# Eight sample states of a decoder layer: outer products on TensorE, or scaled copies on ScalarE and one addition on VectorE

## The chip, the cores and the metric

The kernel runs on one core of one Trainium2 chip. The metric is the device time of one execution in microseconds (us); smaller is better. A core has TensorE (PE in the profile, its weight loads PEld), VectorE (DVE), ScalarE (ACT), GpSimd (POOL) and SyncE (SP), each with its own queue of instructions that run in order. They meet at semaphores only. Data lie in SBUF (128 partitions) and in PSUM, where TensorE writes; DMA queues move data between memory and SBUF.

## The reference, cut to what matters

One layer of a hybrid decoder runs on a prompt of 256 tokens and on 8 samples of one new token each. For the samples the recurrence is a single step per head (8 heads, state 128x128, `f`, `k`, `q` and `v` of 128 numbers per head and sample):

```python
q = silu(q_raw) * 128 ** -0.5
fg = lb + (1 - lb) * sigmoid(f_raw)
k = 1 - fg
S_new = fg[:, None] * S + k[:, None] * v[None, :]     # one state per head and sample
o = q @ S_new
```

`S_new` for all 8 samples and 8 heads is an output (4 MB), and `o` goes on into the head's norm, the gate, the output projection and the rest of the layer.

## The kernel before, in words

All products are made from float32 split into two float16 halves: ScalarE makes the high half of a weight block (L610), VectorE the low half (L977), and TensorE adds three products per pair of tiles. The weights stream through in blocks of 512 KB: SyncE loads a block into one of 4 raw slots, ScalarE and VectorE split it into one of 8 slots, TensorE uses it. ScalarE and VectorE split block `b + 4` in their turn for block `b` (`AHEAD = 4`). Blocks 0 to 79 are the input projection (`S_IN`): ten groups of 8 blocks, each group four tiles of 128 columns for all 264 tokens, 24 products of 0.11 us per block. Group 0 and 3 give q, 1 and 4 f (and k), 2 and 5 v, 6 and 7 the gate g, 8 and 9 u. In a group's last block (7, 15, 23, 31, 39, ...) `evict_in` takes the four tiles out of PSUM: for f, q and g ScalarE makes the sigmoid (`gates`, L621 to L625) and VectorE the product (L1139, L1140, L1145, L1148); the first product of the next group needs the tile of that number free (or, after f, its sigmoid made).

Beside this stream the mixer is woven in, by block numbers. `QUAD_AT = (17, 41)` starts the prompt recurrence of heads 0 to 3 and 4 to 7: every second block TensorE makes the scores of one level (L2081), for which VectorE multiplies q and k (`level`, L1168) and ScalarE packs the keys (`pack_keys`, L717); at +9 and +11 v is turned (L2041), at +16 to +22 follow cross scores, keys, outputs o (L2120, taken by L749 and L751) and final states (L2133, L756, stored by L759). `SAMPLE_AT = (26, 38, 50, 58)` starts the sample states of a pair of heads. With `r` the blocks since then:

- `sample_halves` (VectorE, blocks 24 and 48) splits k and v of the samples into halves in `kv_wide`, four float16 columns of each, and q into `q16`.
- r = 0: TensorE turns them (`sample_kv`, 8 turns of L2030, one between two stream products), ScalarE copies the result to `kv_smp` (L768).
- r = 2 and 4: TensorE makes 8 outer products of four rows each (`outer`, L2055) in two PSUM banks; VectorE makes `state * f + product` (`pair_states`, L1187), 8 instructions of 128x128.
- r = 5 and 6: ScalarE makes the high half of the new state (L776), r = 6 and 7: VectorE the low half (L1280); r = 10: TensorE the 32 small products with q (`os`, L2169 and L2170).
- GpSimd stores the new state and loads that of the next pair into the same two buffers.

Jobs beside the stream share four PSUM banks in turn; the table `JOBS` says who empties each. In_jobs of a block stand behind its sixth stream product. After o of the last pair: mean (L1410), root on ScalarE (`ROOT_AT = 65`, with a table load, L825), Newton step, `o_normalised` (L1320) and the turn of o at blocks 68, 70, 72 and 74 (L2210).

## Time and profile before

| | |
|---|---|
| median of 3 runs | 1169.81 us (1169.33 to 1170.16) |
| the profiled execution | 1170.06 us, of which span 1168.2 us, granted clock 0.998 |
| busy: PE, PEld | 1156.9, 1037.3 us |
| busy: DVE, ACT, POOL | 1006.4, 565.1, 55.5 us |
| L977, low half of a block, on DVE | 414 times, 1.22 us; two in a row start 1.14 us apart |
| L610, high half, on ACT | 414 times, 1.05 us |
| L1187, state times f plus product, on DVE | 64 times, 17.2 us in all |
| L759, issue of a store on ACT's queue; L825, table load | 0.43 us; 1.28 us |
| mean DMA rate | 201 GB/s |

How to read it: PE is an engine that is busy nearly all the time, so what matters of the others is when each delivers. An instruction's duration reaches from its start to its end, but two in a row overlap by some 0.1 us: what a string of them costs is the distance between starts. The span begins with the first instruction of the program; the profiled execution's own time holds 1.9 us around it.

### The profile page before, as it was taken

The numbers are of one execution on the slowest core, as the hardware profiler recorded it, in microseconds if no ns is written. First come the engines' busy times: TensorE is split into PE (matmuls) and PEld (weight loads), VectorE is DVE, ScalarE is ACT, GpSimd is POOL, SyncE is SP. The second block draws the span as 40 slices with busy tenths as digits, with TensorE's granted clock in tenths as the row PEclk, the third lists the DMA queues.
The fourth block names the chain that finished last, engine by engine and source line by source line (L and its number), as shares of the span: only waits on it lengthen the run. The fifth ranks groups of instructions, "written<-read, shape, count | busy, mean of one in ns | idle before, by whom it ended". The sixth has DMA issues, their size and how long they took to land.

```text
span 1168.2 us, 31003 instructions
## 1 busy us (share of the span) xinstructions
PE 1156.9 (99%) x12469; PEld 1037.3 (89%) x12469; DVE 1006.4 (86%) x1575; ACT 565.1 (48%) x810; POOL 55.5 (5%) x80
## 2 busy tenths in 40 slices
PE   8999999999999999999999999999999999999997
PEld 7888888888888899899998999989989999999886
DVE  6778799778867898998989989888899999998687
ACT  6545645654546644444444444444444444444443
POOL 2122310100000200000000000000000000000000
PEclk9999999999999999999999999999999999999999
DMA  8767876766566566666666666666666666667561
GB/s 253 238 200 207 237 217 192 232 190 190 181 211 199 180 216 199 195 194 204 215 200 195 194 202 215 203 193 194 201 199 215 202 199 207 206 199 242 163 190 75
DMA packets 193385, 234.92 MB, mean 201 GB/s; under 512 B 8010, under 2 KB 153777, under 8 KB 193040
## 3 DMA queue, kind: packets, MB, share of 16 engines
q1 hardware_dynamic: 187984, 221.08, 60.4%
q0 software_dynamic: 3968, 11.89, 3.6%
q8 instruction: 53, 0.87, 0.3%
q10 hardware_dynamic: 1360, 0.92, 0.3%
q14 instruction: 20, 0.16, 0.0%
HBM read 226.89 MB, written 7.43 MB: 201 GB/s over the span
## 4 chain that ended last, share of the span: by engine, by line
PE 93%; DVE 4%; ACT 1%; issue 1%; DMA 0%; DVEq 0%; ACTq 0%
PE acc L2322 13%; PE acc L1924 10%; PE acc L1926 10%; PE acc L1928 10%; PE acc L2363 7%; PE acc L2325 6%; PE acc L2324 6%; PE acc L2303 6%; PE acc L2305 6%; PE wrk L2303 4%; PE wrk L2305 4%; PE acc L2365 2%; PE acc L2366 2%; DVE hl L977 2%; PE wrk L2081 1%
## 5 line engine op out<-in xcount | busy, mean ns | idle before, releaser
L977 DVE SCALAR_TENSOR_TENSOR hl<-raw,hl 128x1024 f16<-128x1024 f32 x414 | 493.7, 1220 | 51.7 <-ACT hl L610 49.0
L610 ACT ACTIVATE hl<-raw 128x1024 f16<-128x1024 f32 x414 | 420.3, 1051 | 168.8 <-DMA raw<-in_w_down_dram 88.0
L2322 PE MATMUL acc<-nrm,hl 128*128 128x264 f16 x1344 | 274.8, 276 | 0.3 <-DVE tg L1481 0.3
L1926 PE MATMUL acc<-nrm,hl 128*128 128x264 f16 x920 | 253.9, 276 | 0.0
L1928 PE MATMUL acc<-nrm,hl 128*128 128x264 f16 x920 | 253.9, 276 | 0.0
L1924 PE MATMUL acc<-nrm,hl 128*128 128x264 f16 x920 | 253.9, 276 | 0.0
L2324 PE MATMUL acc<-nrm,hl 128*128 128x264 f16 x672 | 185.5, 276 | 0.0
L2325 PE MATMUL acc<-nrm,hl 128*128 128x264 f16 x672 | 185.5, 276 | 0.0
L2322 PEld LDWEIGHTS acc<-nrm,hl 128*128 128x128 f16 x1344 | 129.0, 98 | 18.1 <-DVE tg L1481 0.6
L2363 PE MATMUL acc<-big,hl 128*128 128x264 f16 x704 | 130.2, 276 | 0.0
L1924 PEld LDWEIGHTS acc<-nrm,hl 128*128 128x128 f16 x920 | 90.2, 98 | 13.2 <-issue 0.3
L1928 PEld LDWEIGHTS acc<-nrm,hl 128*128 128x128 f16 x920 | 90.3, 98 | 12.8
L1926 PEld LDWEIGHTS acc<-nrm,hl 128*128 128x128 f16 x920 | 90.3, 98 | 12.4
L2363 PEld LDWEIGHTS acc<-big,hl 128*128 128x128 f16 x704 | 66.9, 98 | 8.8
L2325 PEld LDWEIGHTS acc<-nrm,hl 128*128 128x128 f16 x672 | 65.8, 98 | 9.8
L2324 PEld LDWEIGHTS acc<-nrm,hl 128*128 128x128 f16 x672 | 65.8, 98 | 9.5
L1924 PE MATMUL acc<-mix,hl 128*128 128x264 f16 x256 | 70.7, 276 | 0.7 <-DVE hid L1357 0.7
L2365 PE MATMUL acc<-big,hl 128*128 128x264 f16 x256 | 70.7, 276 | 0.0
L2366 PE MATMUL acc<-big,hl 128*128 128x264 f16 x256 | 70.7, 276 | 0.0
L1928 PE MATMUL acc<-mix,hl 128*128 128x264 f16 x256 | 70.7, 276 | 0.0
L1926 PE MATMUL acc<-mix,hl 128*128 128x264 f16 x256 | 70.7, 276 | 0.0
L876 ACT ACTIVATE xe<-wrk 128x132 f32<-128x132 f32 x21 | 5.9, 282 | 109.5 <-PE acc L2305 109.5
(492 smaller groups left out, 2241.9 us busy)
## 6 DMA issues: line engine op xcount, KB each, us to landing
raw<-in_w_gate_up_dram SPq DMA_DIRECT2D x168, 512.0 KB, 4.6
raw<-in_w_down_dram SPq DMA_DIRECT2D x88, 512.0 KB, 4.0
raw<-in_w_in_dram SPq DMA_DIRECT2D x80, 512.0 KB, 4.7
raw<-in_w_out_dram SPq DMA_DIRECT2D x32, 512.0 KB, 5.0
raw<-in_w_ple_gate_dram SPq DMA_DIRECT2D x32, 512.0 KB, 5.0
state<-in_state_hgrn_dram POOLq DMA_DIRECT2D x8, 512.0 KB, 6.6
out_new_hgrn_sample_dram<-state POOLq DMA_DIRECT2D x8, 512.0 KB, 5.3
raw<-in_w_gate_up_dram SPq DMA_DIRECT2D x16, 256.0 KB, 3.8
```

The costliest lines, as they stand in the source:

```text
L610: nc.scalar.activation(hi[:, st.hl_slot(j, half), :], raw[:, st.raw_slot(j), :], ACT.Copy, scale=WSCALE).then_inc(hi_done, 1)
L977: stt(lo[:, st.hl_slot(j, half), :], raw[:, st.raw_slot(j), :], WSCALE, hi[:, st.hl_slot(j, half), :], ALU.mult, ALU.subtract).then_inc(lo ...
L1924: mm(out, wh, x_hi[:, kt, :], start=first, stop=False)
L1926: mm(out, wh, x_lo[:, kt, :], start=False, stop=False)
L1928: last = mm(out, wl, x_hi[:, kt, :], start=False, stop=final)
L2303: mm(out, left(0, a), right(1, a), start=begin and a == 0 and out is b.p1, stop=False, skip_group_check=True)
L2305: last = mm(out, left(1, a), right(0, a), start=False, stop=end and a == 1, skip_group_check=True)
L2322: mm(out, wh, n_hi[:, kt, :], start=jj == 0 and kk == 0, stop=False, skip_group_check=bool(up))
L2324: mm(out, wh, n_lo[:, kt, :], start=False, stop=False, skip_group_check=bool(up))
L2325: last = mm(out, wl, n_hi[:, kt, :], start=False, stop=jj == 3 and kk == 3, skip_group_check=bool(up))
L2363: mm(out, wh, ff_hi[:, kt, :], start=j == 0 and kk == 0, stop=False, skip_group_check=True)
L2365: mm(out, wh, ff_lo[:, kt, :], start=False, stop=False, skip_group_check=True)
```

## The change

The new states are made without TensorE. VectorE packs v of four heads and 8 samples side by side (`vs_pack`), TensorE turns the 32 columns once (`sample_values`, blocks 25 and 49, `ROWS_AT`), ScalarE copies the 32 rows out and writes them to a place in memory (`v_rows`); from there one load per head copies the head's 8 rows of 128 numbers to all 128 partitions (`rows_to_all`, into `v_bc`, two buffers). At r = 0 to 3 ScalarE makes one set of 8 scaled copies per block, in place: `state * f` and `v_bc * k`, per partition and sample, each of the two for both heads (for even pairs the state first, for odd pairs v first). VectorE adds the two (`new_states`, r = 3 and 4, one instruction of 128x1024 per head). Everything that follows waits for `state_new` instead. The start blocks are now 27, 38, 51 and 60, and with them the later steps; the clears of `kv_wide` are gone, and those of `win` stand behind the last store.

```diff
-SAMPLE_AT = (26, 38, 50, 58)
-BUF_AT, U_LAST_AT, OSS_AT = 44, (73, 81), 71
-RMS_AT, ROOT_AT, SAMPLE_ROOT_AT = 64, 65, 72
-O_NORM_AT, O_MIX_AT, SAMPLE_MIX_AT = (66, 67, 69, 71), (68, 70, 72, 74), 75
+SAMPLE_AT = (27, 38, 51, 60)
+ROWS_AT = (25, 49)
+BUF_AT, U_LAST_AT, OSS_AT = 44, (73, 81), 73
+RMS_AT, ROOT_AT, SAMPLE_ROOT_AT = 64, 65, 74
+O_NORM_AT, O_MIX_AT, SAMPLE_MIX_AT = (66, 67, 69, 71), (68, 70, 72, 74), 76
...
+    if _b in ROWS_AT:
+        JOBS += [(f"vs_{ROWS_AT.index(_b)}", "act")]
     for _p in range(PAIRS):
         _r = _b - SAMPLE_AT[_p]
-        if _r == 0:
-            JOBS += [(f"kv_{_p}", "act")]
-        elif _r in (2, 4):
-            JOBS += [(f"ou_{_p}_{_r - 2 + j}", "dve") for j in range(2)]
-        elif _r == 10:
+        if _r == 10:
...
-        kv_smp = xe[:, 0:512].bitcast(F16).rearrange("p (s h j d) -> p s h j d", s=2, h=2, j=2)
+        vs_tok, vs_pack = xe[0:4 * NSAMP, 0:P], xe[:, P:P + 4 * NSAMP]
+        v_bc = [xe[:, n:n + 1024].rearrange("p (b v) -> p b v", b=NSAMP) for n in (3136, 2048)]
+        v_rows = nc.dram_tensor("v_rows", (QUADS, 4 * NSAMP, P), F32, kind="Internal").ap()
...
-        kv_wide = [xe[:, n:n + 1024].bitcast(F16).rearrange("p (s c r) -> p s c r", s=2, r=32) for n in (3136, 1024)]
...
-            nc.gpsimd.memset(scores[:, 0:2], 0.0)
-            nc.gpsimd.memset(kv_wide[0], 0.0)
-            for n in range(2):
-                last = nc.gpsimd.memset(win[n][:, :, 0:WPAD], 0.0)
-            last.then_inc(zero_ready, 1)
+            nc.gpsimd.memset(scores[:, 0:2], 0.0).then_inc(zero_ready, 1)
...
-                    pool.wait_ge(drained["dve"], drain_of(f"ou_{p}_3")[1])
+                    pool.wait_ge(state_new, h + 1)
...
-                    pool.wait_ge(job_done, job_value("sb"))
-                    nc.gpsimd.memset(kv_wide[1], 0.0).then_inc(zero_ready, 1)
...
+            for n in range(2):
+                last = nc.gpsimd.memset(win[n][:, :, 0:WPAD], 0.0)
+            last.then_inc(zero_ready, 1)
...
+            def value_rows(c, r):
+                if r == 0:
+                    wait_job(f"vs_{c}")
+                    nc.scalar.activation(vs_tok, wrk[0:4 * NSAMP, JOB[f"vs_{c}"] % JOB_BANKS, 0:P], ACT.Copy)\
+                        .then_inc(drained["act"], 1)
+                    act.wait_ge(drained["act"], drain_of(f"vs_{c}")[1])
+                    act.dma_start(v_rows[c], vs_tok).then_inc(vs_out, 16)
+                elif r == 1:
+                    act.wait_ge(vs_out, 16 * (c + 1))
+                    for h in range(2):
+                        rows_to_all(4 * c + h)
+            def rows_to_all(h):
+                n = NSAMP * P
+                src = bass.AP(v_rows.tensor, v_rows.offset + h * n, [[0, P], [1, n]])
+                act.dma_start(v_bc[h % 2].rearrange("p b v -> p (b v)"), src).then_inc(v_bc_in[h % 2], 16)
             def sample_part(p, r):
-                if r == 0:
-                    wait_job(f"kv_{p}")
-                    if p:
-                        wait_job(f"ou_{p - 1}_3")
-                    nc.scalar.activation(kv_smp, wrk[:, JOB[f"kv_{p}"] % JOB_BANKS, :].bitcast(F16)
-                                         .rearrange("p (s h j d) -> p s h j d", s=2, h=2, j=2), ACT.Copy)\
-                        .then_inc(drained["act"], 1)
+                if r in range(4):
+                    h, old = 2 * p + r % 2, r // 2 == p % 2
+                    x, gains = (state[:, h % 2], f_all) if old else (v_bc[h % 2], k_all)
+                    if old:
+                        act.wait_ge(state_in[h % 2], 16 * (p + 1))
+                        act.wait_ge(acc_free, TPG * (3 * (p // 2) + 3))
+                    else:
+                        act.wait_ge(v_bc_in[h % 2], 16 * (p + 1))
+                    for b in range(NSAMP):
+                        last = nc.scalar.activation(x[:, b, :], x[:, b, :], ACT.Copy, scale=gains[:, h, SEQ + b:SEQ + b + 1])
+                    last.then_inc(state_kept if old else kv_ready, 1)
                 elif r in (5, 6):
                     h = 2 * p + r - 5
-                    act.wait_ge(drained["dve"], drain_of(f"ou_{p}_3")[1])
+                    act.wait_ge(state_new, h + 1)
                     if p:
                         wait_job(f"os_{p - 1}")
                     nc.scalar.activation(s_hi[h % 2], state[:, h % 2], ACT.Copy).then_inc(s_hi_ready, 1)
+                    if p % 2 == 0:
+                        rows_to_all(h + 2)
...
-            def pair_states(p, bs):
-                for h in range(2):
-                    dve.wait_ge(state_in[h], 16 * (p + 1))
-                for bb in bs:
-                    name = f"ou_{p}_{bb}"
-                    wait_job(name)
-                    for n in range(4):
-                        h, b = n // 2, 4 * (n % 2) + bb
-                        s = state[:, h, b, :]
-                        last = stt(s, s, f_all[:, 2 * p + h, SEQ + b:SEQ + b + 1], bank(name)[:, n * P:(n + 1) * P],
-                                   ALU.mult, ALU.add)
-                    drain(last, name)
+            def new_states(h):
+                dve.wait_ge(state_kept, h + 1)
+                dve.wait_ge(kv_ready, h + 1)
+                tt(state[:, h % 2], state[:, h % 2], v_bc[h % 2], ALU.add).then_inc(state_new, 1)
             def sample_halves(c):
-                hs, wide = slice(4 * c, 4 * c + 4), kv_wide[c]
+                hs = slice(4 * c, 4 * c + 4)
                 dve.wait_ge(acc_free, TPG * (3 * c + 3))
-                dve.wait_ge(zero_ready, c + 1)
+                nc.vector.tensor_copy(vs_pack.rearrange("p (h b) -> p h b", h=4), v_all[:, hs, SEQ:TOK]).then_inc(vs_packed, 1)
                 q_s = q_all[:, hs, SEQ:TOK]
                 link(ts(q16[:, hs, :, 0], q_s, Q_UP, None, ALU.mult))
                 stt(q16[:, hs, :, 1], q_s, Q_UP, q16[:, hs, :, 0], ALU.mult, ALU.subtract).then_inc(q16_ready, 1)
-                src = [x[:, hs, SEQ:TOK].unsqueeze(3).to_broadcast([P, 4, NSAMP, 2]) for x in (k_all, v_all)]
-                wide = [wide[:, n].rearrange("p (h b) r -> p h b r", h=4) for n in range(2)]
-                nc.vector.tensor_copy(wide[0][:, :, :, 0:2], src[0])
-                link(nc.vector.tensor_copy(wide[1][:, :, :, 0:4:2], src[1]))
-                tt(wide[0][:, :, :, 2:4], src[0], wide[0][:, :, :, 0:2], ALU.subtract)
-                tt(wide[1][:, :, :, 1:4:2], src[1], wide[1][:, :, :, 0:4:2], ALU.subtract).then_inc(kv4_ready, 1)
...
-                if r in (2, 4):
-                    pair_states(p, (r - 2, r - 1))
+                if r in (3, 4):
+                    new_states(2 * p + r - 3)
...
-            def sample_kv(p):
-                pe.wait_ge(kv4_ready, p // 2 + 1)
-                out = job(f"kv_{p}").bitcast(F16)
-                for n in range(8):
-                    at = 16 * (p % 2) + 4 * (n % 4)
-                    last = nc.tensor.transpose(out[:, n * P:(n + 1) * P],
-                                               kv_wide[p // 2][:, n // 4, at:at + 4, :].rearrange("p c r -> p (c r)"),
-                                               ident16[:])
-                    if n == 7:
-                        last.then_inc(job_done, 1)
-                    yield
+            def sample_values(c):
+                pe.wait_ge(vs_packed, c + 1)
+                out = job(f"vs_{c}")
+                nc.tensor.transpose(out[0:4 * NSAMP, 0:P], vs_pack, ident[:]).then_inc(job_done, 1)
+                yield
...
-            def outer(p, bs):
-                if bs[0] == 0:
-                    pe.wait_ge(drained["act"], drain_of(f"kv_{p}")[1])
-                for bb in bs:
-                    out = job(f"ou_{p}_{bb}")
-                    rows = slice(32 * bb, 32 * bb + 4)
-                    for n in range(4):
-                        last = mm(out[:, n * P:(n + 1) * P], kv_smp[rows, 0, n // 2, n % 2, :],
-                                  kv_smp[rows, 1, n // 2, n % 2, :], start=True, stop=True)
-                    last.then_inc(job_done, 1)
...
-                if r == 0:
-                    yield from sample_kv(p)
-                elif r in (2, 4):
-                    outer(p, (r - 2, r - 1))
-                    yield
-                elif r == 10:
+                if r == 10:
...
+                if b in ROWS_AT:
+                    yield from sample_values(ROWS_AT.index(b))
```

How the instructions move on ScalarE, blocks 27 to 31 (`L717` packs keys, `L610` is the split, `L727` takes v, `L625` the sigmoid of q). Before:

```order
L717 ACTIVATE a<-big 128x8x32 x2
L610 ACTIVATE hl<-raw 128x1024
L727 ACTIVATE mix<-wrk 128x512
L610 ACTIVATE hl<-raw 128x1024
L717 ACTIVATE a<-big 128x4x64 x2
L610 ACTIVATE hl<-raw 128x1024
L625 ACTIVATE gate_t<-acc 128x264 x4
```

With the change (there `L715`, `L608`, `L725` and `L623`; `L790` are the scaled copies):

```order
L715 ACTIVATE a<-big 128x8x32 x2
L790 ACTIVATE state<-state,big 128x128 x8
L608 ACTIVATE hl<-raw 128x1024
L725 ACTIVATE mix<-wrk 128x512
L790 ACTIVATE state<-state,big 128x128 x8
L608 ACTIVATE hl<-raw 128x1024
L715 ACTIVATE a<-big 128x4x64 x2
L790 ACTIVATE xe<-xe,big 128x128 x8
L608 ACTIVATE hl<-raw 128x1024
L790 ACTIVATE xe<-xe,big 128x128 x8
L623 ACTIVATE gate_t<-acc 128x264 x4
```

Four sets of eight scaled copies now stand between the packing of block 27 and the sigmoids of block 31.

On VectorE, blocks 40 to 43 (`L1240` is the product q times f, `L977` the split, `L1211` takes the diagonal, `L1445` turns x, `L1168` is the level). Before:

```order
L1187 SCALAR_TENSOR_TENSOR state<-state,big,wrk 128x128 x8
L1240 TENSOR_TENSOR big<-big 128x4x256
L977 SCALAR_TENSOR_TENSOR hl<-raw,hl 128x1024
L1211 COPY_PREDICATED mix<-masks,wrk 128x512 x2
L977 SCALAR_TENSOR_TENSOR hl<-raw,hl 128x1024
L1187 SCALAR_TENSOR_TENSOR state<-state,big,wrk 128x128 x8
L1445 STREAM_TRANSPOSE hid<-big 128x2x256
L1168 TENSOR_TENSOR big<-big 128x4x64 x4
```

With the change (there `L1251`, `L1002`, `L1222`, `L1457`, `L1193`; `L1206` is the addition of a head):

```order
L1251 TENSOR_TENSOR big<-big 128x4x256
L1002 SCALAR_TENSOR_TENSOR hl<-raw,hl 128x1024
L1206 TENSOR_TENSOR state<-state,xe 128x1024
L1222 COPY_PREDICATED mix<-masks,wrk 128x512 x2
L1002 SCALAR_TENSOR_TENSOR hl<-raw,hl 128x1024
L1206 TENSOR_TENSOR state<-state,xe 128x1024
L1457 STREAM_TRANSPOSE hid<-big 128x2x256
L1193 TENSOR_TENSOR big<-big 128x4x64 x4
```

Each set of eight became one addition, and it moved behind the split of the next block.

## Rows read from the trace of the kernel before

**Rows 1.** The page, part 1: busy time, share of the span, instructions.
```profile
PE 1156.9 (99%) x12469; PEld 1037.3 (89%) x12469; DVE 1006.4 (86%) x1575; ACT 565.1 (48%) x810; POOL 55.5 (5%) x80
```

**Rows 2.** Table of stretches: busy us (instructions) by engine; clock, DMA share, GB/s.
```profile
149.20:216.90 67.70, 67.70 (x685) 60.02 (x685) 67.36 (x137) 36.69 (x62) 9.41 (x10) 1.00 0.74 222
```

**Rows 3.** Timeline of TensorE: start us, us, engine line op out<-in, count.
```profile
97.26 0.28 PE L1928 MATMUL acc<-nrm,hl 128*128 128x264 f16 x1
97.38 0.22 PE L2030 MATMUL wrk<-ident,xe 128*128 128x128 f16 x1
97.43 0.28 PE L1924 MATMUL acc<-nrm,hl 128*128 128x264 f16 x1
...
104.26 0.28 PE L1926 MATMUL acc<-nrm,hl 128*128 128x264 f16 x1
104.47 0.41 PE L2055 MATMUL wrk<-xe 4*128 4x128 f16 x8
104.81 0.29 PE L1928 MATMUL acc<-nrm,hl 128*128 128x264 f16 x1
```

**Rows 4.** Timeline of ScalarE: what an instruction costs.
```profile
14.57 0.31 ACT L669 ACTIVATE nrm<-mix 128x128 f16<-128x128 f32 x1 [0.54 <-DVE mix L1079]
14.79 0.71 ACT L665 ACTIVATE big<-xe,gate_t 128x512 f32<-128x512 f32 x1
15.40 0.82 ACT L682 ACTIVATE nrm<-wrk,gm 128x256 f16<-128x256 f32 x2
...
188.07 0.72 ACT L717 ACTIVATE a<-big 128x256 f32<-128x256 f32 x2 [1.64 <-DVE big L1168]
188.70 1.04 ACT L610 ACTIVATE hl<-raw 128x1024 f16<-128x1024 f32 x1
189.65 0.58 ACT L727 ACTIVATE mix<-wrk 128x512 f16<-128x512 f32 x1
190.12 1.04 ACT L610 ACTIVATE hl<-raw 128x1024 f16<-128x1024 f32 x1
```

**Rows 5.** Timelines of ScalarE, VectorE and TensorE, blocks 27 to 32.
```profile
102.79 0.72 ACT L717 ACTIVATE a<-big 128x256 f32<-128x256 f32 x2 [2.16 <-DVE big L1168]
...
113.94 0.39 ACT L625 ACTIVATE gate_t<-acc 128x264 f32<-128x264 f32 x1 [2.32 <-PE acc L1928]
...
114.94 0.56 DVE L1145 SCALAR_TENSOR_TENSOR big<-acc,gate_t 128x128 f32<-128x128 f32 x3
...
116.59 0.28 PE L1924 MATMUL acc<-nrm,hl 128*128 128x264 f16 x1
```

**Rows 6.** Timelines of ScalarE and TensorE, blocks 38 to 40.
```profile
140.26 0.28 ACT L749 ACTIVATE a<-wrk 128x128 f32<-128x128 f32 x1 [1.13 <-PE wrk L2120]
...
141.75 1.05 ACT L768 ACTIVATE xe<-wrk 128x1024 f16<-128x1024 f16 x1
...
144.54 0.28 PE L1924 MATMUL acc<-nrm,hl 128*128 128x264 f16 x1
```

**Rows 7.** Timelines of VectorE, ScalarE and TensorE, blocks 43 to 47.
```profile
158.55 1.39 DVE L1168 TENSOR_TENSOR big<-big 128x256 f32<-128x256 f32 x4
...
167.78 0.72 ACT L717 ACTIVATE a<-big 128x256 f32<-128x256 f32 x2 [3.24 <-DVE big L1168]
...
169.81 0.27 PE L2081 MATMUL wrk<-big,a 128*128 128x128 f32 x1
```

**Rows 8.** Timelines of VectorE and TensorE, blocks 51 and 56.
```profile
186.61 1.43 DVE L1168 TENSOR_TENSOR big<-big 128x256 f32<-128x256 f32 x4
...
200.75 0.28 PE L1924 MATMUL acc<-nrm,hl 128*128 128x264 f16 x1
```

**Rows 9.** Timelines of ScalarE and TensorE, blocks 61 to 68.
```profile
221.61 0.28 ACT L749 ACTIVATE a<-wrk 128x128 f32<-128x128 f32 x1 [4.99 <-PE wrk L2120]
...
229.60 0.28 PE L1924 MATMUL acc<-nrm,hl 128*128 128x264 f16 x1
...
242.10 0.27 PE L2210 MATMUL wrk<-ident,o_tok 128*128 128x128 f32 x1
```

7 lines of the change are left out of this document (6 added, 1 removed).

## The prediction

> **What bounds the kernel now.** I began with the busy shares: TensorE is busy for 99% of the span [rows 1]. The table of stretches then says whether its partners have room: from 149 to 217 us, inside the stage that the change touches, TensorE is busy for all of the 67.70 us and VectorE for 67.36 [rows 2]. So TensorE sets the end, nothing in this stage holds it up, and VectorE follows without a gap. Two consequences. Work taken from TensorE comes off the end one for one, as long as the others deliver in time. And whatever arrives later than TensorE's slack is added to the end, since nothing later can give it back. The sum is therefore the work removed from TensorE minus nothing, plus every place where it now waits.
>
> **What TensorE loses.** A stream product starts 0.11 us after the one before it; with a turn of L2030 between, the next one starts 0.17 us later (97.26 to 97.43), so a turn costs 0.055 us [rows 3]. Four pairs of 8 turns: 1.76 us. Eight outer products of L2055 stretch 0.11 to 0.55 us (104.26 to 104.81), 0.44 us per burst [rows 3]; eight bursts: 3.52. Added are two turns of packed v, which no row shows; between one turn of L2030 (0.06) and two (0.11), I take 0.11 each, 0.22. Net 5.06 us less. With everything else covered: 1170.06 - 5.06 = 1165.0.
>
> **What ScalarE gains.** It loses four copies of L768 (0.91 us from start to start) and gains eight scaled copies of 128x128 for each of 8 heads, twice (state by f, v by k): 128 instructions. The nearest rows: an unscaled 128x128 copy from SBUF lets the next start after 0.22 us (14.57 to 14.79), a scaled one of 128x512 after 0.61 (14.79 to 15.40) [rows 4]. The split of 1024 columns needs 0.95 (188.70 to 189.65) [rows 4]; the line through 0.22 and 0.95 gives 0.54 for 512 columns, so the per-partition scale adds 0.07 to 0.09. That makes 0.22 + 0.07 = 0.29 us a copy, 2.33 for a head, 37 in all. Bounds: 0.22 (the scale costs nothing at this size) to 0.31. The Trainium skill, ScalarE: Activation LUTs, in its section on what ACT_TABLE_LOAD costs, gives 186 ns + 0.833 per column, 93 more for a pointer scale and an overlap of 93 ns between neighbours. By that page one copy would take an estimated 0.293 us, where the lower bound of the rows is 0.22: at 0.22 the sum would be case 1 below, at 0.293 it stays as it is. It is a rule that speaks against 128-column pieces.
>
> In total ScalarE has room, being busy 565 of 1168 us. But a head's copies stand in each of four consecutive blocks (27 to 30, 38 to 41, 51 to 54, 60 to 63), and ahead of evictions that TensorE needs. I follow ScalarE from the last event that is still tied to TensorE to what TensorE waits for. Pieces, start to start: packing the keys 0.63, split 0.95, v or s copy 0.47 [rows 4], a gate 0.29. "Shift" is how much later than before TensorE is.
>
> **A, the q eviction at block 31.** TensorE's shift is +0.11 - 3 x 0.44 = -1.21. Packing in block 27 waits for VectorE's level; it started at 102.79 [rows 5] and now starts at 102.43, as only one turn and 0.44 went ahead of it. From there: 0.63, 2.33, 0.95, 0.47, 2.33, 0.95, 0.63, 2.33, 0.95, 2.33 = 13.9, so the first gate starts at 116.3, where it was 113.94 [rows 5]. Gate 0.39, VectorE's three products 0.56 [rows 5], signalling 0.05: the tile is free at 117.3. TensorE wants it at 116.59 - 1.21 = 115.4 [rows 5]. Stall 1.9; shift +0.7.
>
> **B, the f gates at block 39.** Squares and copy of o_1 start at 140.26 and take 1.49 (to 141.75) [rows 6]; then 0.91 of L768 becomes 2.33, and TensorE is 0.44 earlier for its lost turns. First gate done near 145.2 in the new time; wanted at 144.54 + 0.7 - 0.44 = 144.8 [rows 6]. Stall 0.4; shift +0.7, and -0.2 after the bursts of blocks 40 and 42.
>
> **C, VectorE's levels of the second quad.** After B ScalarE runs without a gap: four gates 1.5, split, final state and its DMA issue 1.1, then head, split, head, split, packing, head, split, so the split of block 42 ends at 158.9. VectorE needs that split, since its additions and splits stand in one queue: split of block 41 from 155.1, addition, diagonal 1.22, split of block 42 not before 158.95 and to 160.1, addition to 161.2, turn of x 0.63, level to 163.2. It was 158.55 + 1.3 = 159.9 [rows 7]: 3.3 later. VectorE has no idle time to catch up [rows 2], though it is spared the two waves of single-sample products. The next packings had slack of 2.8, 1.3 and 0.8; for the second: packed at 167.78 + 0.72, wanted at 169.81 [rows 7]. With a shift of -0.2 at the start the stalls are 0.7, 1.5 and 0.5. Sum 2.7; shift +2.5. This is the term I trust least: it rests on one queue's order.
>
> **D, the g eviction at block 55.** Shift by then 2.5 + 0.11 - 3 x 0.44 = +1.3. VectorE's level in block 51 started at 186.61 [rows 8]; 3.3 later, 0.5 less for the four wide operations that go: 189.4, done 190.8. ScalarE then has the string of A, 13.9: gate at 204.7, tile free 0.87 later at 205.6. Wanted at 200.75 + 1.3 = 202.0 [rows 8]. Stall 3.6; shift +4.9.
>
> **E, the g eviction at block 63.** o_2 is taken at 221.61 [rows 9], shifted by 4.9 - 0.88 - 0.8 (the 16 products of os_2 now stand behind it) = 3.2, so at 224.8; then 1.49, 2.33, 0.95, 1.49, 2.33: gate at 233.4, tile free 234.25. Wanted at 229.60 + 3.6 = 233.2 [rows 9]. Stall 1.1; shift +4.7.
>
> **F, the first turn of o at block 68.** From that gate: four gates, split, final state with DMA 1.1, head, two splits, high half 0.95 (now in block 65 ahead of the root), table load 1.28, root, split; then VectorE's split, its low half (moved from block 65 to 66, 1.14), Newton step 0.6, scaling 0.8. End near 248.0. Wanted at 242.10 + 4.7 - 0.8 = 246.0 [rows 9]. Stall 2.0.
>
> **Costed at nothing.** The eight loads that copy a head's rows to all partitions, 512 KB each, ride on a DMA share of 0.74 [rows 2]; they have two blocks or more to land, and if they don't, it adds to A or D. Two of them in block 26 and the write of v wait on ScalarE for memory: between packing (96.7) and the next one (102.4) it has 5.7 us for 2.4 us of copies and splits and 1.4 of issues, leaving 1.9 us minus the last bit of the write's flight. No row has so small a write on this queue; the list of DMA issues has small stores (32 to 64 KB) landing after 2.9 to 4.4 us, and part of that lies beside the split and the copy of v. I take no delay, at most 0.8. The Trainium skill, DMA: Bandwidth & Descriptors, section on the anatomy of one DMA (the path of GpSimd), puts about 2.0 us on any DMA's completion; by that page there would be no delay either. VectorE loses 64 products (17 us) and gains eight additions (9): a relief that arrives behind ScalarE's splits and so buys TensorE nothing. GpSimd's two clears move behind the last state and have ten blocks.
>
> **Sum.** Stalls 1.9 + 0.4 + 2.7 + 3.6 + 1.1 + 2.0 = 11.7; less 5.06: +6.6. The profiled execution took 1170.06, the median of the runs is 1169.81; 1170.06 + 6.6 = 1176.7, and I say 1176.5, between the two bases. About 0.2%, 2.3 us, is what a measurement of this kernel can tell from no change.
>
> **Rivals.** (1) *Everything is covered*: ScalarE's copies run at 0.22 or less. Two heads and two heads around the packing of block 29 shorten A by 32 x 0.07 = 2.2, more than its stall; the lag in C falls under the slack; a rest of up to 2 us in D and F stays. Time 1165.0 to 1167. For it: ScalarE is idle half of the time. Against: the row at 15.40. It turns on the price of a copy and decides for faster below about 0.24 us. Chance 0.15. (2) *Half covered*: at 0.25 us a copy, A falls by 1.3, B to nothing, and C, D and F by as much again each through the chain; my sum gives +2: 1172. Chance 0.15. (3) *The stalls as worked out*: 1176.5. Chance 0.53. (4) *More than that*: the row loads or the write land late (0.8 in A, as much in D), or the granted clock, 1.00 throughout this stage [rows 2], falls to the lower level in a wait such as D's; a block of 24 products takes 2.70 us at the high level and would take 5.40 at the low one. One to two such blocks give 1179 to 1182. Chance 0.17. That the freed slots of TensorE's queue are refilled can be left out: the jobs that move (os, oss) are as long as before.
>
> **Chances.** Faster by over 0.2%: case 1, 0.15. Within: most of case 2, 0.12. Slower: 0.73. The range must leave out at most 0.2: low 1168.0 drops case 1 and keeps case 2, high 1183.0 keeps case 4.
>
> **What would show it.** In the new profile: the scaled copies of 128x128 start 0.29 apart; TensorE's waits list the q, g and g evictions (blocks 31, 55, 63) with 1 to 4 us each, packed keys with about 1 us, and the turn of o with 2; VectorE's busy time falls by some 9 us, ScalarE's grows by over 30; before block 27 and after block 70 nothing changes. I am wrong if TensorE still has no wait in this stage (case 1), or if waits are there but on a DMA.

## The result, and the profile after

The changed kernel takes 1181.61 us (median of 4 runs, 1180.14 to 1183.60); the kernel before, run beside it, 1169.95 (1169.33 to 1170.16). The ratio is 1.0097, 95% interval 1.0085 to 1.0109: 11.7 us or 1.0% slower. The forecast was 1176.5 with a range up to 1183.0, and slower as the likeliest sign. The median lies in the stretch of rival 4 (1179 to 1182). The profiled execution took 1183.6 us with a span of 1181.7, where before it was 1170.06 and 1168.2.

The engines' busy times in the page's first part, against [rows 1]:

```profile
PE 1156.6 (98%) x12375; PEld 1035.2 (88%) x12375; DVE 999.0 (85%) x1513; ACT 597.1 (51%) x936; POOL 51.9 (4%) x78
```

ScalarE has 32 us more, VectorE 7 less. TensorE executes 94 recorded instructions fewer and is yet busy for as long as before: some of its products ran slower, as the stretches further down show. In the stretch of [rows 2] VectorE is no longer busy without a gap, ScalarE is at 50 where it was at 37, and TensorE stands still for 6 us:

```profile
149.20:216.90 67.70, 61.62 (x571) 54.26 (x572) 58.13 (x104) 50.05 (x126) 5.89 (x7) 1.00 0.68 206
```

TensorE's waits from 90 to 300 us (for whose tile, and who released it; us in total, times, longest). Before, the same view has one row of 0.7 us:

```profile
PE acc L1936 <- DVE big L1170: 3.5, 1, 3.5
PE acc L1936 <- DVE big L1173: 2.9, 2, 1.8
PE wrk L2075 <- ACT a L715: 2.7, 4, 1.2
PE wrk L2199 <- DVE o_tok L1332: 2.1, 1, 2.1
PE wrk L2040 <- DVE xe L1212: 2.0, 2, 1.8
PE acc L1936 <- ACT gate_t L621: 0.5, 1, 0.5
```

From top to bottom: the q eviction of block 31, the g evictions of blocks 55 (1.8) and 63 (1.1), packed keys (blocks 31, 45, 47 and 49), the first turn of o, the packed v that the change adds, and the f gates. None is on a DMA. Together 13.7 us, and 5.06 were taken away: that is 8.6, where the blocks together became 13.2 longer. Of the 4.6 that are left, 3.4 are in the granted clock, in two stretches right behind the two longest waits (columns as in [rows 2]: window, its length, busy time and count of TensorE, its weight loads, VectorE, ScalarE and GpSimd, then granted clock, DMA share, GB/s):

```profile
119.70:124.10 4.40, 4.36 (x24) 3.23 (x25) 4.40 (x16) 3.91 (x5) 0.33 (x1) 0.61 0.62 226
250.00:257.20 7.20, 5.06 (x31) 3.72 (x29) 7.10 (x17) 1.98 (x3) 0.00 (x0) 0.76 0.85 257
```

In the first, the 24 products of block 32 take 4.36 us where a block of them takes 2.70: from 120.5 us on they start 0.22 us apart in place of 0.11, the lower of the clock's two levels (1.2 in place of 2.4 GHz).

The length of a block, from its first stream product to that of the next, shows where the time is (us, profiled executions; worked out from the start times in TensorE's timeline):

```
block     25    31    32    39    45    47    49    55    63    68    83
before  3.58  3.58  2.70  4.04  3.61  3.58  3.58  3.58  4.05  3.94  3.53
after   4.05  8.06  4.36  4.68  4.46  5.03  6.19  5.57  5.31  7.14  2.70
```

The sum over all blocks from 20 to 84 is +13.2 us in the profiled execution. The medians differ by less (11.7), as this execution was the slowest of the four.

Place A shows how a wait comes about. ScalarE around blocks 25 to 31:

```profile
96.51 0.32 ACTq L767 DMA_DIRECT2D v_rows<-xe  x1
96.94 1.06 ACT L608 ACTIVATE hl<-raw 128x1024 f16<-128x1024 f32 x1 [0.46 <-ACT xe L764]
97.90 0.58 ACT L725 ACTIVATE mix<-wrk 128x512 f16<-128x512 f32 x1
101.41 2.27 ACTq L777 DMA_DIRECT2D xe<-v_rows  x2
103.78 1.06 ACT L608 ACTIVATE hl<-raw 128x1024 f16<-128x1024 f32 x1 [5.30 <-issue]
104.74 0.71 ACT L715 ACTIVATE a<-big 128x256 f32<-128x256 f32 x2
105.36 2.43 ACT L790 ACTIVATE state<-state,big 128x128 f32<-128x128 f32 x8
107.70 1.04 ACT L608 ACTIVATE hl<-raw 128x1024 f16<-128x1024 f32 x1
...
118.63 0.37 ACT L623 ACTIVATE gate_t<-acc 128x264 f32<-128x264 f32 x1
```

A string of eight scaled copies holds ScalarE for 2.34 us (105.36 to 107.70), 0.29 a copy. But ahead of them ScalarE issues the write of v (96.51), makes a split and a copy, stands still from 98.48 until 101.41, when the write has landed, and then spends 2.27 us on issuing two loads. Its packing starts at 104.74 (forecast 102.43) and the first gate at 118.63 (forecast 116.3).

### The profile page after: what moved, and what is told of

It reads as the page before. It is cut to its first block, busy times and chain, and to the rows that moved or that the text cites. A ratio compares the mean times of both kernels' runs of the same rounds, so it can differ in the third digit from the quotient of the medians.

```text
span 1181.7 us, 30885 instructions
## 1 busy us (share of the span) xinstructions
PE 1156.6 (98%) x12375; PEld 1035.2 (88%) x12375; DVE 999.0 (85%) x1513; ACT 597.1 (51%) x936; POOL 51.9 (4%) x78
## 4 chain that ended last, share of the span: by engine, by line
PE 85%; ACT 6%; DVE 5%; issue 2%; DMA 2%; ACTq 0%; DVEq 0%; SPq 0%
PE acc L2313 13%; PE acc L1936 10%; PE acc L1940 9%; PE acc L1938 9%; PE acc L2315 6%; PE acc L2316 6%; PE acc L2354 6%; PE acc L2294 5%; PE acc L2296 5%; PE wrk L2294 4%; PE wrk L2296 4%; PE acc L2357 2%; PE acc L2356 2%; DVE hl L1002 2%; ACT state L790 1%
## 5 line engine op out<-in xcount | busy, mean ns | idle before, releaser
L1002 DVE SCALAR_TENSOR_TENSOR hl<-raw,hl 128x1024 f16<-128x1024 f32 x414 | 494.1, 1220 | 70.4 <-ACT hl L608 67.5
L608 ACT ACTIVATE hl<-raw 128x1024 f16<-128x1024 f32 x414 | 420.6, 1052 | 183.5 <-DMA raw<-in_w_down_dram 93.6
L1940 PEld LDWEIGHTS acc<-nrm,hl 128*128 128x128 f16 x920 | 90.9, 99 | 13.2
```

Of the source, the lines that this page charges most:

```text
L608: nc.scalar.activation(hi[:, st.hl_slot(j, half), :], raw[:, st.raw_slot(j), :], ACT.Copy, scale=WSCALE).then_inc(hi_done, 1)
L1002: stt(lo[:, st.hl_slot(j, half), :], raw[:, st.raw_slot(j), :], WSCALE, hi[:, st.hl_slot(j, half), :], ALU.mult, ALU.subtract).then_inc(lo ...
L1940: last = mm(out, wl, x_hi[:, kt, :], start=False, stop=final)
```

## Experiments

The **theory** is that of the prediction: ScalarE's strings stand ahead of evictions and packings, each late delivery stops TensorE, and nothing gives it back. **Rivals**: v's trip through memory is the cause; the moved block numbers are; VectorE's queue is. I follow TensorE's shift, how much later it starts a block than in the kernel before (us, worked out as above, and set to zero at block 20):

```
block                      31    34    40    45    50    57    64    69    72    85
the change               -0.9   5.3   5.5   4.6   9.5  10.1  10.1  13.3  13.9  13.2
one copy per head        -0.9  -0.9  -1.3  -2.2  -0.1  -1.4  -2.7  -2.5  -1.2  -1.9
trip on GpSimd's queue   -0.9   1.2   1.5   0.6   5.6   6.3   6.2   7.7   9.0   8.4
filled waits             -0.9   2.7   2.9   2.0   6.9   7.5   7.4   8.9  10.3   9.6
behind the eviction      -0.9   1.7   1.9   1.0   5.9   6.2   6.1   9.3  10.0   9.3
moved numbers alone       0.0   0.0   0.0   0.0   0.0   0.0  -0.4   1.3   2.6   1.9
states by VectorE        -0.9   0.9   1.1   0.2   5.6   5.9   4.6   5.5   6.8   6.1
keys by GpSimd           -0.9   1.0   0.6  -0.3   3.8   3.9   3.5   4.4   5.7   5.0
keys by GpSimd, later    -0.9  -0.4   0.2  -0.7   1.3   0.2   0.2   1.1   2.4   1.8
low half behind          -1.2  -1.0  -0.5  -1.4   0.8   0.1  -0.5  -0.8   1.7   1.0
both by GpSimd           -1.2  -1.2  -1.7  -2.6  -0.7   0.5  -0.9   0.0   2.4   1.8
strings spread           -1.2  -0.6   1.9   1.0   1.7   2.2   4.0   4.7   6.8   6.2
first quad only          -1.2  -0.5  -1.0  -1.9   0.1   0.6   0.6   0.6   0.6  -0.2
```

**One copy per head.** The change with shorter strings.

```diff
-for b in range(NSAMP):
-    last = nc.scalar.activation(x[:, b, :], x[:, b, :], ACT.Copy, scale=gains[:, h, SEQ + b:SEQ + b + 1])
+last = nc.scalar.activation(x, x, ACT.Copy, scale=gains[:, h, SEQ:SEQ + 1])
```

> Each string of eight scaled 128x128 copies (2.33 us of ScalarE) becomes one scaled copy of 128x1024 (about 0.95 us, as the splits of 1024 columns), so ScalarE holds back 1.38 us less in each of sixteen places. All samples of a head are scaled by the first sample's f or k: that part of the recurrence is left out. Theory (the length of ScalarE's strings ahead of evictions and packings is what makes TensorE wait): the waits on the q, g and g evictions and on o fall to under 1 us in all but the first place, where the 2.3 us for the issues and the wait on memory remain; 1166 to 1169 us. Rival (the trip of v through memory, its transfers and issues): the waits stay, 1178 to 1182 us.

1168.87 us, ratio to before 0.9988 (0.9980 to 0.9997). All its waits from 90 to 300 us:

```profile
PE wrk L2039 <- DVE xe L1211: 2.0, 2, 1.8
PE wrk L2198 <- DVE o_tok L1331: 0.8, 1, 0.8
PE acc L1935 <- ACT big L699: 0.5, 1, 0.5
```

The waits on q, g, g, f and the packed keys are gone, the one on o falls from 2.1 to 0.8, and the clock is 1.00 throughout. The trip through memory is still there (the write takes 4.4 us, the two loads 0.8 to issue) and no wait of TensorE comes of it: the rival falls as a cause of its own. 21 us less on ScalarE (1.3 in each of sixteen places) make 12.7 us of time. What stays is packed v in block 49, 1.8 us. From block 45 on each removed burst shows: TensorE is 2.2 us ahead at block 45 and 2.7 at block 64, with the 1.8 lost in between.

**Trip on GpSimd's queue.** The strings stay, the queue changes.

```diff
-act.dma_start(v_rows[c], vs_tok).then_inc(vs_out, 16)
-act.wait_ge(vs_out, 16 * (c + 1))
+pool.wait_ge(drained["act"], drain_of(f"vs_{c}")[1])
+pool.dma_start(v_rows[c], vs_tok).then_inc(vs_out, 16)
+pool.wait_ge(vs_out, 16 * (c + 1))
...
```

> Write of v and loads of the rows leave ScalarE's queue for GpSimd's, which is idle nine tenths of the time; the strings stay on ScalarE. Theory (strings are the main cause, the trip adds its 2.3 us in the first place and through a wait of 3.5 us a fall of the granted clock): the wait on the q eviction falls from 3.5 to about 1.2 us and block 32 runs at the upper level of the granted clock again, 4 us less there; the g eviction of block 55 takes back 1 to 2 us, since TensorE comes there sooner: 1177 to 1180 us. Rival (trip is the main cause): more than half of the 11.7 us comes back, 1175 us or less.

1179.12 us, ratio 1.0075 (1.0062 to 1.0088), as expected; the wait on q, expected at about 1.2, is 1.9, and the one on g in block 55 stays at 1.8. ScalarE:

```profile
102.83 0.72 ACT L731 ACTIVATE a<-big 128x256 f32<-128x256 f32 x2 [3.51 <-DVE big L1195]
...
116.74 1.20 ACT L639 ACTIVATE gate_t<-acc 128x264 f32<-128x264 f32 x4
```

Packing at 102.83 and the gate 13.91 us later: the prediction's chain of 13.9 to the digit. The clock does not fall behind the wait on q, nor behind one of 2.2 us on o. In the change, then, v's trip made block 31 longer by 2.4 us: 1.5 in the wait on q, the rest at the packed keys before it. In the profiled executions the two kernels are 4.8 us apart at block 85, 3.3 of it from the clock in blocks 32 and 68; the medians differ by 2.5 only, so the other executions of the change may have lost less to the clock, which no run here shows block by block.

**Filled waits.** Idle products (`repeats` issues n products into a free bank).

```diff
+if st is S_IN and i == 4 and n == 0:
+    repeats("cr_0", 30)
 pe.wait_ge(acc_free, t - (TPG - 1))
...
 out = job(f"ot_{j}")
+if j == 0:
+    repeats("ot_0", 18)
```

> TensorE executes 30 products of no use (128x264, 3.3 us) ahead of its wait on the q eviction at block 32, and 18 (2.0 us) ahead of the wait on o at block 68, into a PSUM bank that nobody reads. Theory (the granted clock fell in blocks 32 and 68 because TensorE had stood still for 3.5 and 2.1 us): the waits vanish in the trace, both blocks run at 1.00, and 1.7 + 1.9 us come off: 1177.5 to 1179 us. Rival (the clock falls for another reason, or fill runs too long): the blocks stay slow or the products push the end: 1181 to 1183 us.

1179.87 us, 1.7 less than the change and 0.9 above what I expected at most. The two medians come from different sets of runs, so the blocks say more. Both stretches are at 1.00 now:

```profile
120.00:125.00 5.00, 5.00 (x47) 4.47 (x46) 4.96 (x13) 4.03 (x6) 1.31 (x2) 1.00 0.53 161
250.00:257.00 7.00, 6.96 (x78) 5.94 (x77) 5.38 (x11) 1.59 (x3) 0.00 (x0) 1.00 0.69 217
```

Block 32 is back at 2.71 us (from 4.36) and block 68 at 5.42 (from 7.14); at block 85 the shift is 3.6 less: 3.4 from these two, 0.9 because the row loads took 0.84 us to issue here and block 31 had no wait on packed keys, less 0.7 lost in block 71. The fall was worth 1.7 us in each place of the profiled execution. At q the gate comes at 117.98 and TensorE's own work ends at 115.46, so without the fill it would have waited about 3.6 us, as long as in the change; there the fill is the likely reason that the clock stayed up. At o it is not shown: with a wait of 2.2 us and no fill the clock stayed up in the kernel above.

**Behind the eviction.** Pairs 0 and 2, the fourth string one block later.

```diff
+if p % 2 == 0 and r in (3, 4):
+    r = 7 - r
...
-if r in (3, 4):
-    new_states(2 * p + r - 3)
+if r in ((3, 5) if p % 2 == 0 else (3, 4)):
+    new_states(2 * p + (r > 3))
```

> In pairs 0 and 2 the fourth string of scaled copies moves behind the eviction (block 31 in place of 30, block 55 in place of 54), and the addition of the second head one block later; nothing else changes. Theory: the q eviction comes 2.33 us sooner, its wait falls from 3.5 to 1.1 us and the granted clock stays up in block 32 (4.0 us less in all); the g eviction of block 55 waits no longer (2.0), but what TensorE gains there meets the next late delivery, block 63 and o, so that 1 to 3 us of it are given back: 1176 to 1179 us. Rival (order on ScalarE is not what matters, the transfers are): 1180 to 1183 us.

1180.61 us (1178.15 to 1184.26), ratio 1.0091 (1.0078 to 1.0105): less was won than expected, and the time is in the rival's range. The first gate came at 114.89, 3.74 us sooner than in the change (2.33 for the string, the rest because the two row loads took 0.84 us to issue and not 2.27), yet the wait on q is 2.4 and not 1.1. VectorE:

```profile
115.01 1.23 DVE L1004 SCALAR_TENSOR_TENSOR hl<-raw,hl 128x1024 f16<-128x1024 f32 x1 [1.89 <-ACT hl L608]
116.16 1.22 DVE L1208 TENSOR_TENSOR state<-state,xe 128x1024 f32<-128x1024 f32 x1
117.29 1.96 DVE L1172 SCALAR_TENSOR_TENSOR big<-acc,gate_t 128x128 f32<-128x128 f32 x12
```

Its share of the eviction stands behind a split and the first addition of block 30, 2.28 us: with ScalarE in time, VectorE's order is the next to be late. And behind the wait of 2.2 us on o the clock fell again (0.78 from 250 to 257 us), which takes back 1.7.

**Moved numbers alone.** The kernel before, fourth pair and sums at the change's blocks.

```diff
-SAMPLE_AT = (26, 38, 50, 58)
+SAMPLE_AT = (26, 38, 50, 60)
...
```

> The kernel before with only the block numbers of the last part moved as the change moves them (fourth pair 58 to 60, the sums and roots of the samples 71, 72, 75 to 73, 74, 76); outer products and turns stay on TensorE. Theory (the 2.1 us wait on o comes from the scaled copies, the moves alone cost little): 1169.5 to 1171.5 us, wait on o under 1 us. Rival (the moved high half and low half ahead of the scaling of o make the wait, whatever the recurrence is computed by): wait of 1.5 to 2 us at the first turn of o, 1172 us or more.

1172.02 us, ratio 1.0017 (1.0008 to 1.0026): the rival. With no scaled copy anywhere TensorE waits on o for nearly as long as in the change:

```profile
PE wrk L2210 <- DVE o_tok L1320: 1.9, 1, 1.9
```

VectorE makes the first low half in block 66 (240.39) ahead of the Newton step and the scaling of o (242.15). It still has the single-sample products here (2.15 us a string), which the change has replaced by additions, so this run does not yet say what makes the 2.1 us there.

**States by VectorE.** ScalarE keeps v by k.

```diff
-tt(state[:, h % 2], state[:, h % 2], v_bc[h % 2], ALU.add).then_inc(state_new, 1)
+for b in range(NSAMP):
+    s = state[:, h % 2, b, :]
+    last = stt(s, s, f_all[:, h, SEQ + b:SEQ + b + 1], v_bc[h % 2][:, b, :], ALU.mult, ALU.add)
+last.then_inc(state_new, 1)
...
```

> ScalarE keeps only v by k (one string of 2.33 us per head in place of two); state by f and the sum go back to VectorE, 8 single-sample products per head (2.1 us in place of 1.14 for the addition). Theory (ScalarE's strings are the larger part): half of the strings go, VectorE has some 1 us more per head; the q and g evictions come 2 to 4 us sooner, the rest stays: 1171 to 1175 us. Rival (VectorE's queue, full from 149 to 217 us, is what is late): its longer products keep the waits where they are, 1179 us or more.

1177.46 us, ratio 1.0060 (1.0047 to 1.0074), between the two theories. Half of the strings gone take the wait on q from 3.5 to 1.6 and that on g in block 55 from 1.8 to 1.5, and that on g in block 63 (1.1) is gone; packed keys (2.6), packed v (1.8) and o (1.5) stay. The 2.1 us of products on VectorE, where one addition took 1.14, ate part of what ScalarE gave: the wait on packed keys in block 45 grew from 0.6 to 1.1.

**Keys by GpSimd**, with no scaled copies on ScalarE.

```diff
+nc.gpsimd.tensor_tensor(x, x, k_all[:, h, SEQ:TOK].unsqueeze(2).to_broadcast([P, NSAMP, P]), ALU.mult)\
+    .then_inc(kv_ready, 1)
...
```

> No scaled copy on ScalarE at all: GpSimd writes v, loads its rows to all partitions and multiplies by k (one product of 128x1024 per head, gains repeated along v; from its 128x264 products of 0.82 to 1.02 us about 3.2 to 3.9 us each), VectorE multiplies by f and adds as before the change (8 products per head). Theory: with ScalarE's strings and its two row loads gone the q, g and g evictions are in time; what stays is the wait for packed v in block 49 (1.8 us, VectorE's place for it) and up to 1 us at o: 1166 to 1169 us. Rival (GpSimd is too slow or disturbs VectorE when both work): VectorE waits for the products, 1171 us or more.

1176.86 us, ratio 1.0059 (1.0045 to 1.0073): the rival. GpSimd, and VectorE at the same time:

```profile
107.17 3.93 POOL L559 TENSOR_TENSOR xe<-xe,big 128x1024 f32<-128x1024 f32 x2 [0.49 <-DMA xe<-v_rows]
```

```profile
108.25 3.80 DVE L1199 TENSOR_TENSOR big<-big 128x256 f32<-128x256 f32 x4 [1.62 <-PE wrk L2084]
```

GpSimd is quicker than I took it to be (1.96 us a product), but VectorE's four level products, 1.42 us elsewhere, take 3.80 beside it.

**Keys by GpSimd, later.** v's turn in block 50, products of pairs 0 and 2 one block later.

```diff
-ROWS_AT = (25, 49)
+ROWS_AT = (25, 50)
...
-if r in (3, 4):
+if r in ((4, 5) if p % 2 == 0 else (3, 4)):
```

> As the kernel with GpSimd's products, but v of the second quad is turned and written one block later (50 for 49), and VectorE's products of pairs 0 and 2 come one block later. Theory (the wait of 1.8 us in block 49 is only that VectorE packs v behind the samples' outputs, in the same block in which TensorE turns it): it disappears, 1.8 us less than that kernel, 1164.5 to 1167 us. Rival (VectorE is so far behind by then that the next wait takes it over): the same time within 0.5 us.

1172.29 us, ratio 1.0017 (1.0008 to 1.0026). 4.6 us less than the kernel above, though not as low as expected. The wait of 1.8 on packed v went (the 0.2 of block 25 stays), and so did those on q (1.7) and g (1.3), since VectorE's products now stand behind the evictions. Left are packed keys 1.8, o 1.5, two of 0.5 in blocks 61 and 71 and, in blocks 35 and 59, turns that wait 1.3 in all for VectorE.

**Low half behind, and both by GpSimd.** Two kernels on top of that one: GpSimd packs v, the last low halves stand behind the scaling of o; and in the second GpSimd multiplies the states too, and VectorE only adds.

```diff
+nc.gpsimd.tensor_copy(vs_pack.rearrange("p (h b) -> p h b", h=4), v_all[:, 4 * c:4 * c + 4, SEQ:TOK])\
+    .then_inc(vs_packed, 1)
...
                     o_normalised(h + 1)
+                if b - SAMPLE_AT[-1] in (6, 7):
+                    state_low(b - SAMPLE_AT[-1])
```

```diff
+nc.gpsimd.tensor_tensor(x, x, f_all[:, h, SEQ:TOK].unsqueeze(2).to_broadcast([P, NSAMP, P]), ALU.mult)\
+    .then_inc(state_kept, 1)
...
```

> As the last kernel with GpSimd's product by k and VectorE's single-sample products, with v turned in block 49 again but packed by GpSimd, and with the two low halves of the last pair's states behind the scaling of o in blocks 66 and 67. Theory (the wait of 1.5 us on o is VectorE's low half of the last pair, which the moved block numbers put ahead of the scaling): it goes, and the wait on packed v stays away, 1169.5 to 1171.5 us, against 1172.3. Rival (VectorE arrives late at o because of its products in blocks 63 and 64): the wait stays over 1 us, 1171.5 to 1173 us.

> As the kernel beside it, but GpSimd multiplies the states by f too (16 products of 128x1024 in all, 1.96 us each by the trace of its first kernel), and VectorE has one addition per head (1.14 us) in place of eight products (2.1 us), some 8 us less in all. Theory (what is left of TensorE's waits, on packed keys in blocks 45 and 47 and on VectorE's blocks, is VectorE's lateness in the full stretch from 149 to 217 us): the waits sum to under 1.5 us and nearly all of TensorE's 5.06 us shows, 1165.5 to 1168 us, faster than the kernel before. Rival (GpSimd's products and VectorE's operations lengthen each other, or GpSimd's queue becomes late): 1169.5 us or more.

The first: 1171.95 us, 1.0015 (1.0006 to 1.0024), the same as the kernel above within its interval. The wait on o fell from 1.5 to 0.4: in these kernels it was the low half's 1.14 us. The next delivery is late in its place, u's eviction in block 71:

```profile
PE acc L1963 <- ACT big L744: 1.6, 1, 1.6
...
PE wrk L2226 <- DVE o_tok L1357: 0.4, 1, 0.4
```

The second: 1172.47 us, 1.0018 (1.0009 to 1.0027); the rival. At block 45 it is 2.6 us ahead, the most of all: each burst removed shows in full up to there. Then it loses all, 1.1 and 0.9 us of it on packed keys in blocks 53 and 55. GpSimd, and VectorE beside it:

```profile
97.93 3.76 POOL L566 TENSOR_TENSOR state<-state,big 128x1024 f32<-128x1024 f32 x2
```

```profile
98.00 4.78 DVE L1027 SCALAR_TENSOR_TENSOR hl<-raw,hl 128x1024 f16<-128x1024 f32 x1
...
184.18 4.11 DVE L1027 SCALAR_TENSOR_TENSOR hl<-raw,hl 128x1024 f16<-128x1024 f32 x1
```

A split that takes 1.22 us takes 4.78 when two GpSimd products run: it ends 1.1 us after they do (102.78 and 101.69), as if it had begun only then. At 98 us no wait of TensorE comes of it; behind 184 us come the waits of blocks 53 and 55.

**Strings spread.** The change's method, best places I could find.

```diff
+STRINGS = ((0, 1, 2, 4), (-3, -2, 2, 3), (0, 1, 2, 4), (-1, 0, 2, 3))
...
```

> The changed method whole (all scaled copies on ScalarE, additions on VectorE), only placed otherwise: v's write and row loads on GpSimd's queue, v packed by GpSimd; of each pair the strings moved away from evictions (pairs 0 and 2: fourth string behind the eviction of block 31 or 55, both additions behind it too; pair 1: v's strings in blocks 35 and 36, when ScalarE has little to do; pair 3: in 59 and 60); the last low halves behind the scaling of o. Theory (the loss is in where the strings stand, not in ScalarE's total of 37 us): no wait on q, none on f; g of block 55 at most 1.3, levels 1 to 2, g of 63 and o under 1 us each, so about 3 to 4 us of waits against 5.06 taken away: 1168 to 1171 us, with all of ScalarE's 37 us still there. Rival (the amount of ScalarE's work is what is too much): 1174 us or more.

1177.84 us, ratio 1.0055 (1.0042 to 1.0069). What concerns pair 0, the keys and packed v held: q 0.5 us, packed keys 0.3 in all, packed v none. For pair 2 the wait on g in block 55 is 1.7 where I allowed 1.3. The part about pairs 1 and 3 failed. ScalarE:

```profile
132.69 2.45 ACT L805 ACTIVATE xe<-xe,big 128x128 f32<-128x128 f32 x8 [4.32 <-DMA xe<-v_rows]
...
138.39 2.44 ACT L805 ACTIVATE xe<-xe,big 128x128 f32<-128x128 f32 x8 [1.82 <-DMA xe<-v_rows]
```

The strings came ahead of their rows, ScalarE stood still for 6.1 us with splits and gates queued behind, and the f gates cost TensorE 2.8 us in block 39; in the fourth pair it is the same again (1.0 and 2.7 us for the rows), block 63 being 3.1 us longer than before. The 1.5 us by which block 64 is longer are the granted clock, which fell behind this wait of 2.9 us and not behind the 2.8 in block 39:

```profile
233.00:238.00 5.00, 4.58 (x28) 3.45 (x29) 3.66 (x6) 4.47 (x14) 0.71 (x1) 0.66 0.40 91
```

So this run does not tell whether ScalarE's 37 us can be placed without loss.

**First quad only.** The kernel before, with GpSimd's products for pairs 0 and 1 and the outer products kept for 2 and 3.

```diff
-if r == 0:
-    yield from sample_kv(p)
-elif r in (2, 4):
+if r == 0 and p > 1:
+    yield from sample_kv(p)
+elif r in (2, 4) and p > 1:
...
```

> The kernel before, with the outer products and turns taken from TensorE for the first quad alone (pairs 0 and 1), where VectorE still has idle time; the second quad keeps outer products and block numbers of before. Packing of v, the trip through memory and v by k are GpSimd's, state by f of pair 0 too; VectorE has two additions for pair 0 and its single-sample products for pair 1; ScalarE has no scaled copies. TensorE loses four bursts of 0.44 and two sets of turns of 0.44 and gains one turn of 0.11: 2.5 us less. Theory (the work on TensorE comes off the end wherever the helper has idle time of its own, and the second quad's waits come from VectorE and ScalarE being full there): no wait over 0.5 us that the kernel before lacks, 1167.3 to 1169 us beside 1169.8 of before, faster. Rival (VectorE's levels of the second quad have a slack of only 0.8 to 2.8 us and turn the 2.5 us into waits at blocks 45 to 49): 1169.5 us or more.

1169.76 us (1169.39 to 1171.32). Its ratio to the runs beside it is 0.9989 (0.9980 to 0.9998), but those runs of the kernel before had a median of 1170.85; against the 1169.81 of the first runs nothing is left. I count it as no difference. At block 45 it is 1.9 us ahead, then:

```profile
PE wrk L2144 <- ACT a L755: 1.5, 2, 1.2
```

The packed keys of block 47 take 1.2 of it, and by block 50 it is all gone: the second quad's levels run on VectorE's pace, and here TensorE gains nothing by arriving there sooner. VectorE's pace is not fixed, though. The level that starts at 158.55 before the change [rows 7] starts, in the kernel with one copy per head and in this one:

```profile
157.02 1.40 DVE L1192 TENSOR_TENSOR big<-big 128x256 f32<-128x256 f32 x4
```

```profile
159.20 1.40 DVE L1215 TENSOR_TENSOR big<-big 128x256 f32<-128x256 f32 x4
```

With additions for pair 1 (1.22 us a head) it is 1.5 us sooner and no packing is late; with single-sample products (2.19 a head) it is 0.7 later.

## Why the prediction was right, and where it was not

**TensorE's loss, 5.06 us.** It holds for each piece: the blocks with one burst are 0.44 shorter in every kernel that drops it, and at block 31 the shift is -0.9 where I had -1.2 (packed v in block 25 is the difference: where GpSimd packs it, the shift is -1.2). As a gain it does not hold past block 45 in the first-quad kernel, and it does in the one with one copy per head; "comes off the end one for one, as long as the others deliver in time" was right in its condition. Wrong was that VectorE's relief "buys TensorE nothing": it is true of the change, where it stands behind ScalarE's splits, but with short strings the same additions bring the level forward by 1.5 us, and the packed keys are in time for an earlier TensorE.

**A scaled copy, 0.29.** Measured 0.2925 (2.34 for eight), and rivals 1 and 2 fall with this price. The Trainium skill, ScalarE: Activation LUTs, section on what ACT_TABLE_LOAD costs, gave an estimated 0.293; the trace agrees. The copies of 128x1024, 1.04 us for a head, bring the time back to that of the kernel before or a little under it (1168.87), above the 1165 to 1167 that rival 1 gave for strings of 1.76 or less: packed v and the wait on o stay.

**A.** Forecast 1.9. Without the trip it is 1.9, start to start as worked out. What failed is the sentence "I take no delay, at most 0.8": v's trip cost 2.3 us. The write took 4.9 us from issue to landing, where the nearest rows were 2.9 to 4.4; the two issues took 2.27 where I had counted some 1.4 for three. In block 50 the same trip is short, with 2.0 us from the write's issue to its landing and 0.81 for the two issues:

```profile
190.28 0.33 ACTq L767 DMA_DIRECT2D v_rows<-xe  x1
...
192.26 0.81 ACTq L777 DMA_DIRECT2D xe<-v_rows  x2
```

The Trainium skill's page DMA: Bandwidth & Descriptors, section on the anatomy of one DMA, puts the fixed part of a DMA on GpSimd's path at about 2.0 us; the write of block 50 agrees with it, that of block 26 does not, and the measurement decides. What made the difference stays open.

**B.** Forecast 0.4, block 39 is 0.6 longer. **C.** Forecast 0.7, 1.5 and 0.5; blocks 45 and 47 are 0.85 and 1.45 longer, packed keys in block 49 0.5. The term I trusted least was the closest.

**D.** Forecast 3.6, measured 2.0, and 1.8 us of a wait I had not seen lie before it: TensorE turns v in block 49 while VectorE packs it behind the outputs of the samples. D's chain held: packing at 195.53 and the gate at 209.45, 13.9 later. But the packing came 4.7 us later than forecast (190.8) and TensorE 6.6 later (208.6 for 202.0), so it waited 1.8 less. That packed v's 1.8 us were taken from D's wait one for one is not shown: with the fourth string moved, TensorE waits 1.5 at D behind the wait on packed v and 1.7 without it, in kernels that differ in other places too. The step that failed is that I costed v's turns at their TensorE time only, and did not ask when VectorE would have packed v; the same copy waits 0.2 in block 25.

**E.** Forecast 1.1, measured 1.3.

**F.** Forecast 2.0, measured 2.1, by the chain as it was worked out, though from a shift of 10.1 and not 4.7. Two of its terms can be told apart. One is the last string: with one copy per head, and additions and block numbers as in the change, the wait is 0.8. The last state product on ScalarE and the scaling of o on VectorE, in the change and in that kernel (ScalarE's and VectorE's timelines):

```profile
241.38 2.44 ACT L790 ACTIVATE state<-state,big 128x128 f32<-128x128 f32 x8 [0.53 <-ACT s_final L754]
252.07 0.87 DVE L1332 TENSOR_SCALAR o_tok<-o_tok,rs_o 128x128 f32<-128x128 f32 x4
```

```profile
229.05 1.15 ACT L789 ACTIVATE state<-state,big 128x1024 f32<-128x1024 f32 x1 [0.53 <-ACT s_final L754]
238.44 0.87 DVE L1331 TENSOR_SCALAR o_tok<-o_tok,rs_o 128x128 f32<-128x128 f32 x4
```

From the one to the other it is 10.69 us and 9.39: the string's 1.3 us more are the wait's 1.3 us more. The other is the low half "moved from block 65 to 66", 1.14 us: where it stands behind the scaling the wait falls from 1.5 to 0.4. The kernel with the moved numbers alone comes to 1.9 without a string, with single-sample products on VectorE where the change has additions.

**The clock**, rival 4, chance 0.17: it came, and not behind D, but behind A and F, 1.7 us in each, and the median lies in that rival's stretch and not in that of the likeliest case. With what is above, in the profiled execution: -5.1 + A 1.9 + trip 2.3 + B 0.6 + C 2.8 + packed v 2.0 + D 2.0 + E 1.3 + F 2.1 + clock 3.4 = 13.3. Block 83 is 0.8 shorter, as a wait that the kernel before has there (0.7) disappears; that is 12.5, against 13.2 found. The stalls as forecast, 11.7, measured 10.7. The forecast for the profiled execution was 1176.7 and it took 1183.6: 6.9 more, of which the trip, packed v and the clock make 7.7, the smaller stalls and block 83 take back 1.8, and 1.0 stays open. The median, 1181.6, is 2.0 below that execution, and how its parts differ no run shows. So the sign and the places of most waits came from the mechanism forecast. The size did not: the median is within the range because that left room for rival 4, and that the room held packed v too, which no case named, is luck.

## What to carry to other kernels

Work taken from the engine that sets the end is worth only what the others' next deadlines leave: take each delivery's slack from the trace before pricing the removal, since in the first-quad kernel two packings, 1.2 us at the first, gave back what had been won. A short string of instructions on an engine that is idle for half of the time can cost its full length where a delivery stands behind it in the same queue (the last one, 1.3 us shorter, gave back 1.3 at the first turn of o), but need not (the fourth one moved away gave back 1.1 of 2.3 at q), and moving it can make it worse if its own input isn't there yet. When something new is handed over between engines, ask of every hand-over, the smallest too, where in its maker's queue it is made: 32 columns of packed v cost TensorE 1.8 us, as much as the g eviction of block 55.
